# A second expert beside the first: 64 rows on two column tiles, or 32 rows on four

## The reference

```python
def _moe_swiglu(x, w_router, w_gate, w_up, w_down):
    logits = (xf @ w_router).astype(jnp.float32)
    top_logit, top_idx = lax.top_k(logits, TOP_K)          # TOP_K = 2
    top_w = jax.nn.softmax(top_logit, axis=-1)
    ...
    def expert_block(args):
        xs, e = args
        return (jax.nn.silu(xs @ w_gate[e]) * (xs @ w_up[e])) @ w_down[e]
    ...
    out = jnp.zeros_like(xf).at[row_token].add(y_rows)
```

## Time and profile before

| | us |
|---|---|
| runs of the kernel before | 2260.49, 2261.12, 2264.60 (median 2261.12) |
| profiled execution, its time | 2260.72 |
| its span (first to last instruction) | 2258.8 |
| lies around the span | 1.9 |
| PE busy in the span | 2203.8 (98%) |

### The profile page before, as it was taken

How to read it: one execution, slowest core, us unless ns; L and a number is a source line. 1 busy time by engine, 2 the same in 40 slices (tenths; PEclk the granted TensorE clock), 3 DMA queues, 4 the chain that set the end, 5 groups by cost and what they waited for, 6 DMA issues and landing times.

```text
span 2258.8 us, 41782 instructions
## 1 busy us (share of the span) xinstructions
PE 2203.8 (98%) x16926; PEld 1844.2 (82%) x16926; DVE 1608.3 (71%) x2231; ACT 1196.5 (53%) x1640; POOL 138.5 (6%) x133
## 2 busy tenths in 40 slices
PE   8999999999999999999999999989999999999997
PEld 8998888999888899888888998877786666666665
DVE  5768878677888868987656689869886555554445
ACT  5774655576565564354444643446765444444343
POOL 2200000310000001100000011000000000000000
PEclk9999999999999999999999999989999999999999
DMA  6454555444555443245554432358999999999994
GB/s 236 165 223 171 184 198 175 152 141 169 205 187 186 150 168 132 95 150 214 193 190 157 168 132 95 150 224 331 389 366 400 419 421 421 420 420 381 364 370 187
DMA packets 77646, 536.43 MB, mean 237 GB/s; under 512 B 8976, under 2 KB 9488, under 8 KB 14608
## 3 DMA queue, kind: packets, MB, share of 16 engines
q1 hardware_dynamic: 73520, 517.51, 60.3%
q0 software_dynamic: 3936, 16.25, 1.8%
HBM read 523.51 MB, written 6.82 MB: 235 GB/s over the span
## 4 chain that ended last, share of the span: by engine, by line
PE 86%; DVE 6%; issue 4%; ACT 2%; DMA 1%; POOL 0%; DVEq 0%; SPq 0%; ACTq 0%; POOLq 0%
PE bank L895 17%; PE bank L904 9%; PE bank L942 8%; PE bank L1525 8%; PE bank L906 5%; PE bank L1555 5%; PE bank L997 4%; PE bank L1343 4%; PE bank L1592 3%; PE bank L976 3%; PE bank L1439 3%; PE bank L927 3%; PE bank L1609 2%; DVE w_lo L3397 2%; PE bank L1461 2%
## 5 line engine op out<-in xcount | busy, mean ns | idle before, releaser
L3459 DVE TENSOR_TENSOR w_lo<-ring,w_hi 128x2048 fp32r<-128x2048 f32 x67 | 153.6, 2292 | 156.2 <-ACT w_hi L2292 156.2
L2384 DVE TENSOR_TENSOR w_lo<-ring,w_hi 128x2048 fp32r<-128x2048 f32 x97 | 222.1, 2290 | 54.9 <-ACT w_hi L1749 53.5
L904 PE MATMUL bank<-x_both,w_hi 128*128 128x512 f32 x960 | 239.9, 392 | 0.0
L1749 ACT ACTIVATE w_hi<-ring 128x2048 fp32r<-128x2048 f32 x99 | 189.7, 1918 | 37.9 <-PE bank L942 34.1
L2292 ACT ACTIVATE w_hi<-ring 128x2048 fp32r<-128x2048 f32 x67 | 128.2, 1913 | 137.6 <-DMA ring<-in_stream 130.6
L904 PEld LDWEIGHTS bank<-x_both,w_hi 128*128 128x128 f32 x960 | 174.3, 189 | 32.3
L895 PE MATMUL bank<-x_hi,in_hi 128*128 128x256 f32 x576 | 164.2, 285 | 0.0
L895 PE MATMUL bank<-x_hi,ring_lo 128*128 128x256 f32 x576 | 162.4, 282 | 0.0
L895 PE MATMUL bank<-x_lo,in_hi 128*128 128x256 f32 x576 | 161.3, 280 | 0.0
L2511 DVE TENSOR_TENSOR ring_lo<-ring,in_hi 128x2048 fp32r<-128x2048 f32 x39 | 89.4, 2295 | 85.7 <-ACT in_hi L1788 85.7
L1760 ACT ACTIVATE gates<-bank 128x256 f32<-128x256 f32 x120 | 39.6, 382 | 191.4 <-PE bank L906 191.4
(11 more groups left out here) (596 smaller groups left out, 6155.1 us busy)
## 6 DMA issues: line engine op xcount, KB each, us to landing
ring<-in_stream SPq DMA_DIRECT2D x393, 1024.0 KB, 5.4
yT<-in_stream SPq DMA_DIRECT2D x45, 1024.0 KB, 8.4
xT<-in_stream SPq DMA_DIRECT2D x39, 1024.0 KB, 9.8
Z<-in_stream SPq DMA_DIRECT2D x8, 1024.0 KB, 7.8
norm_rows<-in_rows POOLq DMA_DIRECT2D x4, 1024.0 KB, 7.6
Z<-Z SPq DMA_DIRECT2D x24, 128.0 KB, 2.1
slot_rows<-cst POOLq DMA_DIRECT2D x4, 512.0 KB, 4.3
slot_rows<-gates POOLq DMA_DIRECT2D x4, 512.0 KB, 8.4
```

Of the source, the lines that this page charges most:

```text
L904: mm(two[c], w[0][:, at[k]], x_both[:, :, k, :], start=(k == 0), stop=False)
L1749: act_(part(w_hi, n), slot(f0 + n), ACT.Copy).then_inc(*A.done("hi", f0 + n))
L2384: v.tensor_tensor(part(w_lo, n), slot(f0 + n), part(w_hi, n).bitcast(F32), ALU.subtract)\
L3459: v.tensor_tensor(moe_part(w_lo, at), both_slot("most", at), moe_part(w_hi, at).bitcast(F32), ALU.subtract)\
```

## The change

The few-expert of the last pair (rank 6, the smallest of the ranked) gets a capacity of 32 rows in place of 64, and takes the form that the tail has: four column tiles. In pairs 0 and 1 nothing changes.

- `few_in` in the last pair issues 16 matmuls of 32 rows x 128 columns for 8 of 64 x 256, and `few_down` 8 of 32 x 256 for 4 of 64 x 512. Their loops and waits are the same.
- ACT's silu of the few is 64 columns wide in place of 128. The copies of the turned hidden rows of tail and few (two of 64 partitions for the tail and one for the few) become two that take both.
- The end: `few_hi` and `few_lo` are 256 columns wide in place of 512; DVE makes `pickT_few` as four parts of 256 in place of two; the scatter has 16 matmuls of 256 columns with it in place of 8 of 512.
- In turn 0 the capacity takes one more small DVE instruction, `parts_of` one less. The buffers of few lie at other addresses.

```diff
 for q in range(4):
     k = q + 4 * (kind == "far")
-    w = both_slot("few", i)[:, q * 512:(q + 1) * 512].rearrange("p (g f n) -> p g f n", g=2, f=2)
-    for f in range(2):
-        r = mm(few_up[few_tile(f), :].rearrange("p (g n) -> p g n", g=2),
+    w = both_slot("few", i)[:, q * 512:(q + 1) * 512].rearrange("p (g f n) -> p g f n", g=2, f=parts)
+    for f in range(parts):
+        r = mm(few_up[few_part(d, f), 0:512 // parts].rearrange("p (g n) -> p g n", g=2),
                x_few(d)[:, k, :], w[:, :, f, :], start=(k == 0), stop=(k == KT - 1))
...
+parts = 4 if last else 2
 for c in range(2):
-    for half in range(2):
-        r = mm(few_y[few_tile(half), :], hT_few[:, j % 2, few_tile(c)],
-               both_slot("few", i)[:, c * D + half * 512:c * D + (half + 1) * 512],
+    for f in range(parts):
+        r = mm(few_y[few_part(d, f), 0:D // parts], hT_few(d)[:, j % 2, few_part(d, c)],
+               both_slot("few", i)[:, c * D + f * (D // parts):c * D + (f + 1) * (D // parts)],
                start=(j == 0 and c == 0), stop=(j == FJ - 1 and c == 1))
...
+v.tensor_scalar(more_of, nth_of, 2.0 * DUOS, float(TAIL - FEW), ALU.is_equal, ALU.mult)
...
-for q in range(2):
-    v.tensor_scalar(pickT_few[:, q, :], picked_few, 0.0, parts_of[:, 4 + q:5 + q], ALU.is_gt, ALU.mult)
+for q in range(4):
+    v.tensor_scalar(pickT_few[:, q, :], picked_few, 0.0, parts_of[:, q:q + 1], ALU.is_gt, ALU.mult)
-for q in range(4):
     v.tensor_scalar(pickT_tail[:, q, :], picked_tail, 0.0, parts_of[:, q:q + 1], ALU.is_gt, ALU.mult)
```

More of the change, by code:

```diff
@@ L458, in few_tile, with few_part @@
             return slice(i * FEW, (i + 1) * FEW)
+        def few_part(d, i):
+            return few_tile(i) if d < DUOS - 1 else tail_tile(i)
         tail_up, tail_y, few_up, few_y = banks[2][:, 0:P], banks[3][:, 0:SEQ], banks[5][:, 0:SEQ], banks[7]
@@ L652, in emit @@
         turn_cells = ctx.enter_context(nc.sbuf_tensor("turn_cells", [1, 16], mybir.dt.int32))[:, :]
-        x_few_0, x_few_2 = (par[:, a:a + KT * w].rearrange("p (k n) -> p k n", k=KT) for a, w in ((0, P), (KT * P, FEW + TAIL)))
-        x_tail = x_few_2[:, :, FEW:FEW + TAIL]
+        x_few_0, x_few_2 = (par[:, a:a + KT * w].rearrange("p (k n) -> p k n", k=KT) for a, w in ((0, P), (KT * P, 2 * TAIL)))
+        x_tail = x_few_2[:, :, TAIL:2 * TAIL]
         def x_few(d):
-            return x_few_0[:, :, d * FEW:(d + 1) * FEW] if d < 2 else x_few_2[:, :, 0:FEW]
+            return x_few_0[:, :, d * FEW:(d + 1) * FEW] if d < 2 else x_few_2[:, :, 0:TAIL]
         pick_few = par[:, 1792:1792 + 2 * TB * P].rearrange("p (s b n) -> p s b n", s=2, b=TB)
-        few_hi, few_lo = (rounded(n, a, 512, par_at) for n, a in (("few_hi", 0), ("few_lo", 512)))
+        few_hi, few_lo = (rounded(n, a, SEQ, par_at) for n, a in (("few_hi", 512), ("few_lo", 768)))
         tail_hi, tail_lo = (rounded(n, a, SEQ, par_at) for n, a in (("tail_hi", 1024), ("tail_lo", 1280)))
@@ L664, in emit, with hT_few @@
         act_tail, act_few = par[:, 1792:1792 + 64], par[:, 1856:1856 + P]
-        hid_tail, hid_few, hT_few = (par[:, a:a + 2 * P].rearrange("p (b n) -> p b n", b=2) for a in (1984, 2240, 2496))
-        hT_tail = par[:, 2752:2752 + P].rearrange("p (b n) -> p b n", b=2)
+        hid_tail, hid_few, hT_two = (par[:, a:a + 2 * P].rearrange("p (b n) -> p b n", b=2) for a in (1984, 2240, 2496))
+        hT_both = par[:, 2496:2496 + 2 * P].rearrange("p (e b n) -> p e b n", e=2, b=2)
+        hT_tail = hT_both[:, 0, :, :]
+        def hT_few(d):
+            return hT_two if d < DUOS - 1 else hT_both[:, 1, :, :]
         tail_weight, few_weight = par[:, 2880:2881], par[:, 2888:2889]
-        parts_of = par[:, 2896:2902]
+        parts_of = par[:, 2896:2900]
         few_rows = gates[:, 1024:1024 + 512]
@@ L1676, in pair @@
                         for tb in range(TB):
-                            for y in (few_hi, few_lo):
-                                mm(scattered(tb, half), pickT_few[:, half, tb * P:(tb + 1) * P], y, start=(y is few_hi), stop=False)
                             for q in range(2):
+                                for y in (few_hi, few_lo):
+                                    mm(scattered(tb, half)[:, q * SEQ:(q + 1) * SEQ], pickT_few[:, 2 * half + q, tb * P:(tb + 1) * P], y,
+                                       start=(q == 0 and y is few_hi), stop=False)
                                 for y in (tail_hi, tail_lo):
@@ L2258, in silu @@
                         sc.wait_ge(*T.of(*of_pair(d, "few_unit", MOE_UNIT[("far", j)])))
-                        act_(act_few, few_up[:, 0:P], ACT.Silu).then_inc(*done("few_silu", j))
+                        w = P // 2 if last else P
+                        act_(act_few[:, 0:w], few_up[:, 0:w], ACT.Silu).then_inc(*done("few_silu", j))
                     def hT(j):
@@ L2270, in hT @@
                         act_(hT_hi[:, j % 2, :], turned_most, ACT.Copy).then_inc(*done("hT", j))
[L2271 to L2276, removed]
+                        if not last:
+                            act_(hT_few(d)[:, j % 2, :], turned_few, ACT.Copy).then_inc(*done("hT_few", j))
+                            return
+                        both = banks[6][:, SEQ:2 * SEQ].rearrange("p (e c g n) -> p e c g n", e=2, c=2, g=2)
+                        for g in range(2):
+                            act_(hT_both[64 * g:64 * g + 64, :, j % 2, :].rearrange("p e (c n) -> p e c n", c=2),
+                                 both[64 * g:64 * g + 64, :, :, g, :], ACT.Copy).then_inc(*done("hT_few", j))
                     for half in range(2):
@@ L2314, in pair @@
                     sc.wait_ge(*T.of(*of_pair(d, "few_unit", MOE_UNIT[("down", FJ - 1)])))
-                    act_(few_hi, few_y, ACT.Copy, scale=few_weight).then_inc(*A.done("last_few"))
+                    act_(few_hi, few_y[:, 0:SEQ], ACT.Copy, scale=few_weight).then_inc(*A.done("last_few"))
                     sc.wait_ge(*T.of(*of_pair(d, "tail_unit", MOE_UNIT[("down", FJ - 1)])))
@@ L3369, in find_few @@
                 def find_few():
-                    v.memset(pick_few[:, 1, :, FEW + TAIL:P], 0.0).then_inc(*L.done("pick_few"))
+                    v.memset(pick_few[:, 1, :, 2 * TAIL:P], 0.0).then_inc(*L.done("pick_few"))
                     for tb in range(TB):
-                        for part, a, w, at in [(d // 2, FEW * (d % 2), FEW, FEW_COLUMN + d) for d in range(DUOS)] + [(1, FEW, TAIL, TAIL_COLUMN)]:
+                        for part, a, w, at in ((0, 0, FEW, FEW_COLUMN), (0, FEW, FEW, FEW_COLUMN + 1), (1, 0, TAIL, FEW_COLUMN + 2), (1, TAIL, TAIL, TAIL_COLUMN)):
                             v.tensor_scalar(pick_few[:, part, tb, a:a + w], ct("slots", 0, w), place[:, tb, at:at + 1], sel[:, tb, at:at + 1],
@@ L3448, in hidden @@
                         ve.wait_ge(*A.of(*of_pair(d, "few_silu", j)))
-                        v.tensor_tensor(hid_few[:, j % 2, :], act_few, few_up[:, P:2 * P], ALU.mult).then_inc(*done("few_hidden", j))
+                        if last:
+                            v.tensor_tensor(hid_few[:, j % 2, :].rearrange("p (g n) -> p g n", g=2), grow(act_few[:, 0:64], [P, 2, 64], 1),
+                                            grow(few_up[:, 64:P], [P, 2, 64], 1), ALU.mult).then_inc(*done("few_hidden", j))
+                        else:
+                            v.tensor_tensor(hid_few[:, j % 2, :], act_few, few_up[:, P:2 * P], ALU.mult).then_inc(*done("few_hidden", j))
                     def hT(j):
@@ L3495, in pair @@
                     ve.wait_ge(*A.of("last_few"))
-                    v.scalar_tensor_tensor(out=few_lo, in0=few_y, scalar=few_weight, in1=few_hi.bitcast(F32),
+                    v.scalar_tensor_tensor(out=few_lo, in0=few_y[:, 0:SEQ], scalar=few_weight, in1=few_hi.bitcast(F32),
                                            op0=ALU.mult, op1=ALU.subtract).then_inc(*V.done("last_few"))
```

12 lines of the change are left out of this document (6 added, 6 removed).

## The result

The changed kernel takes 2242.85 us (median of 4 runs, 2240.98 to 2247.93) where the kernel before took 2261.36: a ratio of 0.992 (95% interval 0.990 to 0.994), 18.5 us less. Four more runs beside other kernels gave 2240.19 (ratio 0.990, 0.988 to 0.991). The forecast was 2239, the range 2233 to 2250.

What follows compares the result with a forecast made beforehand. PE was taken to bound the last pair. PE's units -28.7, start +2.5, end +1.3 and loads +3 sum to -21.9 us, giving 2238.8 us (2239.2 beside the median); range 2233 to 2250.

Steps and rivals of the forecast that it cites:

- PE's units: Last pair: 22 `few_in` and 11 `few_down` save 0.87 us each, 28.7 us gross; bound 0.1 us a unit below.
- The loads: Up near of step 2 to down of block 8: loads bind at times and cost 3 us, bounds 0 and 5 to 13.
- The slack of 9.3 us: Last pair's new step: a near unit's load may take 9.3 us from issue before PE waits.
- The start: Steps 0 and 1 of the last pair: PE stays behind DVE's product, 2.5 us given back, 0.9 to 1.0 remain.
- The end: Last `few_down` waits for `hT_lo` of step 10 behind the picks on DVE: 1.3 us given back.
- The loads take the pace: Rival, last pair: loads move only 380 to 405 GB/s, gain 8 to 17 us, say 2249 us; chance 0.17.
- Better than forecast: Rival, last pair: PE gains 0.1 us more a unit and slack hides the loads' excess, 2234 us; chance 0.09.
- No gain: Rival, last pair: loads already bind at 361 GB/s, PE's freed time becomes waiting, 2260 us; chance 0.03.
- The turn's price: Rival, rank 6 with 33 to 64 rows overflows: one more turn of 94.4 us, 2333 us; chance 0.03.

Runs made afterwards that it cites:

- the second profile: The changed kernel run again unaltered, for another profile: 2240.19 us, ratio 0.990 to the kernel before.
- the half-loads run: Changed kernel with only the first half of each few-expert unit loaded in the last pair: 2234.36 us, ratio 0.987 to the kernel before.
- Filling the wait: Changed kernel with 14 small f32 matmuls put into PE's wait ahead of `tail_in` near of step 1 in the last pair: 2244.68 us.
- the new order in all steps: Changed kernel with ACT's silus and DVE's products put ahead of the near unit in all 11 steps of the last pair: 2236.59 us.
- both orders in all steps: Changed kernel with silus and products ahead in all steps of the last pair, and the picks made behind `hT_lo` at its end: 2236.49 us.

## Why the prediction was right, and where its terms were off

*PE's units.* Right for the few's own groups, 0.87 us each. I set the bound at 0.1 us a unit for equal forms side by side and took nothing of it. It is 0.14 us for a group of the tail behind one of the few. A step without a wait went from 17.87 to 14.92 us, 2.95 less, where the few's own groups give 2.61; over 11 steps that is 32 us gross, not 28.7. The prediction also said that no row priced this. One place did: the last two `few_down` of the kernel before stand side by side, and they take 3.59 us to the start of the next group, where two that stand apart take 3.74 (timeline of PE):

```profile
2233.63 1.94 PE L1609 MATMUL bank<-yT,par 128*64 128x512 f32 x8
2235.40 1.89 PE L1609 MATMUL bank<-xT,par 128*64 128x512 f32 x8
2237.22 1.07 PE L1577 MATMUL bank<-ring,par 128*32 128x256 f32 x16
```

*The loads.* The stretch from `up` near of step 2 to `down` of block 8 was forecast at 135.3 us, as 132.3 of PE and 3 of the loads; it took 134.9, and 134.3 in the second profile. The bytes over the rate (56.6 MB at 420 GB/s, 134.8 us) gave the right end, and the 3 us had been chosen near them. The split was wrong. PE alone would have needed 8 x 14.92 + 10.3 = 129.6 us, so the loads' term was about 5 us and not 3. (The 10.3 is what the changed kernel shows; from the forecast's own rows it should have been 10.5.) In the half-loads run the stretch took 130.8 us, of which 1.4 are a lower clock behind its wait ahead of step 2, where `up` near takes 4.35 us for 2.95. The two errors cancel because the loads bind: what PE gained beyond the forecast had nowhere to go. The slack of 9.3 us that I gave a near load was right in kind. In step 5 ACT began to round the load of the next near unit at 2127.23, 11.9 us after `up` near at 2115.34, 2.6 more than the slack, and in that step PE waited 1.5 us for a load of the few and 1.1 for the tail's product.

*The start.* 0.7 us kept in one profile and 0.1 in the other, against 0.9. The step left out the clock: PE stands 3.3 us (2.7) where it stood 1.8, and `up` near of step 1 then takes 4.54 (4.91) us for 2.95. Filling the wait showed that the path, not the clock, would have bounded step 1 all the same. The path begins with a load, and the half-loads run, where step 2 begins 2.2 us earlier, shows that this load is late.

*The end.* This term failed. I gave it 1.3 us saved and it was -0.6 in one profile, +0.3 in the other. The wait behind the picks came nearly as foreseen, 1.5 us for 1.3. But there is another one ahead of it that I had not named, `down_tail` of block 9 for `hT_lo` of step 9 (1.6 and 0.7 us): ACT and DVE reach the last far unit late because its loads are late, a cost of the stretch before, paid after it. The half-loads run shows that it is the loads: there `down_tail` of block 9 does not wait, the wait behind the picks is 1.1 us, and the end takes 33.3 us, 1.7 less than before, where 1.3 was forecast. So the sum gave the loads 3 us in one stretch, and they cost something in all three.

*Ahead of the pair*, 2.4 us of the shortfall of the profiled execution are scatter as far as these runs can tell.

*The rivals.* The loads take the pace: half right, they do, but at 417 to 420 GB/s and not at 380 to 405, so the gain stayed near the forecast. Better than forecast: PE did gain what that rival said, and the loads took it back, which the forecast's sentence on it had said. No gain, and with it the Trainium skill's 358 GB/s for a core (DMA: Bandwidth & Descriptors, "Where 436 GB/s comes from"), is refuted by the windows of the pair itself. The Trainium skill's drain at a change of the tiling mode (TensorEngine Tiling, "Key Properties") fits the 1.01 and 0.87 us of one and the same group, behind another form and behind its own; no run here separates it from other costs of a change of form. The turn's price was right within a microsecond by the stores of rows.

## What to carry to other kernels

When an engine that sets the pace is made faster beside a stream of loads, divide the stretch's bytes by the rate that the same queue shows when it is full: that is the next bound, and it is good to a microsecond in both profiles of the changed kernel here, while the sum over the engine's units was off by more than three. Look then at the short steps at either end of the stretch, where one path through all engines is longer than the engine's own work: there shorter work only lengthens a wait, and an order that lets the dependent step go ahead of the next load gave back 3.7 to 4.7 us of the pair. To tell which of two full engines binds, leave out a part of the bytes: here the same 17 MB cost 1.7 us of the pair before the change and about 8 after it.

## What the runs showed of the hardware

- A group of 16 f32 matmuls of 32 x 128 columns (32 records) takes 1.01 us behind a group of 128-column or 64-column form and 0.87 behind one of its own form.
- After PE had stood still for 3.3 us between groups, the granted clock was 0.80 and then 0.60 in the next windows, 0.50 in the second profile (1.2 GHz throughout, behind a wait of 2.7 us), and 12 matmuls that take 2.95 us took 4.54 and 4.91. With 14 small matmuls in the wait it stayed at 1.00, until the next wait of 1.9 us, behind which it was 0.50.
- The length of one wait does not tell whether the clock falls: it stayed at 1.00 behind 1.8 us in the kernel before and behind 2.0 us in the kernel with the new order in all steps, and fell behind 1.9 us with the filled wait and behind 2.1 us with both orders in all steps.
- The loads of 1 MB into `ring` took 9.9 us from issue to landing (median of the last pair) at a mean rate of 408 GB/s, and 7.3 before the change at 368 GB/s.
